# Pairs of chunks in a macaron encoder: two of four weight sums by accumulating transfers between slots, a bias table gathered in long rows, and later sums on GpSimd

## The chip, the cores and the metric

The kernel runs on one core of one Trainium2 chip. TensorE (PE) multiplies, VectorE (DVE) and ScalarE (ACT) prepare operands and evict results, GpSimd (POOL) does small sums and issues some transfers, SyncE (SP) issues the weight loads. The metric is the time of one execution in microseconds, median over runs. Lower is better.

## What is computed

Two layers, 256 tokens, model width 1024. Each layer has a feed-forward stage, a mixing stage and a second feed-forward stage:

```python
for l in range(DEPTH):
    x = x + 0.5 * swiglu(rms_norm(x, ffn1_norm[l]), ffn1_w_gate[l], ffn1_w_up[l], ffn1_w_down[l])
    h = rms_norm(x, mix_norm[l])
    z = h @ w_in[l]                    # q, k, v of 8 heads, p of 4 pooling groups
    a = neighborhood_attention(q, k, v, rpb[l])      # adds rpb_f[:, dr_idx][:, :, dc_idx], then a column mask
    m = multiscale_pool(p, w_pool[l], pool_scale[l])
    x = x + jnp.concatenate([a, m], axis=-1) @ w_out[l]
    x = x + 0.5 * swiglu(rms_norm(x, ffn2_norm[l]), ffn2_w_gate[l], ffn2_w_up[l], ffn2_w_down[l])
return rms_norm(x, final_norm)
```

with `swiglu(h, wg, wu, wd) = (silu(h @ wg) * (h @ wu)) @ wd`, and a feed-forward width of 2816, which the kernel takes as 11 chunks of 256. All data are float32.

## The kernel before

**Split products.** Every float32 product is made of three products on TensorE: each operand is split into a rounded part ("hi") and the rest ("lo"), and PE computes hi·hi, hi·lo and lo·hi (lines 1382, 1383 and 1385). A weight unit of 128 x 2048 words lies raw in a slot `w_raw[s]`; ACT writes `w_hi[s]` from it (`split_hi`, line 655, two instructions of 1024 words; line 662, four of 512, where a gain is folded in), and DVE subtracts to get `w_lo[s]` (`split_lo`, lines 1009 and 1020). There are five slots: three through the whole kernel, called a, b and d in a feed-forward stage, and e and f in such stages only. SP loads a slot as soon as its last `lo` is done.

**A feed-forward stage** (four of them: FF1 and FF2 of two layers) begins with chunk 0 and 1 in the ordinary way, then runs a loop of two bodies (`ff_body`), each of which handles one ordinary chunk and one *pair* of chunks, and ends with two more chunks. A pair is computed by seven half-size products in place of eight (`seventh` on PE), in the manner of Strassen and Winograd. For that it needs

- sums of the activations, made once a stage by POOL: `x_sums` first adds `xt_hi` and `xt_lo` back to the full value (line 504, two instructions of 1024 words), ACT scales the result by the gains (`scale_x`, line 749, eight instructions, which need both sums) and rounds it (`x_hi`, line 758), DVE makes the rest (`x_lo`, line 1096); then POOL makes four sums of blocks (lines 515 to 524, in place), which ACT and DVE split again (`s_hi`, `s_lo`, line 1107);
- four sums of weights for each pair. With raw units in e, f, b and a: the first sum is `e += f` on DVE (`add_units(e, f)`, line 1123), the second `b += e` on DVE, the third adds b's original words to f: POOL issues two transfers from DRAM that accumulate into slot f (`add_load`, line 532), and the fourth is `a += b` on DVE.

**The order at the start of a stage.** Every engine works through its own instructions in the written order. ACT: the splits of a's and b's second units (chunk 1), the split of d's first unit, `scale_x`, `store_gt_hi` of chunk 0 (line 729), `x_hi`, then chunk 1's silu. DVE: a's second unit, b's second unit (line 1020, four instructions each), d's first unit, `store_gt_lo` of chunk 0 (line 1076), `x_lo`, then chunk 1's gate, the third units of a and b, `s_lo`, and the first unit of the loop. PE: the products of chunk 1, then the down projection of chunk 0, which needs `gt_lo` of chunk 0, then chunk 2 with the scaled activations `xs`, the down projection of chunk 1, and the first `seventh`. POOL starts `x_sums` as soon as the transposed activations are complete (semaphore `xt_lo_ready`).

**The order in a pair.** PE: seventh e, seventh f, seventh a, seventh b, then seventh e with the second sum (called S2 here), a down projection, seventh f with the third sum, seventh a with the fourth, then the ordinary products from e and f. DVE's order around S2 is shown with the change.

**The bias.** The attention bias is 8 heads x 6 row distances x 64 columns per partition. It is gathered from `rpb` by `gather_rows` (line 551) on POOL's queue: 16 transfers a layer whose source runs backwards along the partitions, four heads' transfers in each loop body of FF1 and FF2 of layer 0, into a DRAM scratch; `load_bias` (line 559) fetches it to `bias` after the first feed-forward stage, and DVE applies the mask in place (line 1265).

## Time and profile before

| | |
|---|---|
| median of 3 runs | 937.91 us (934.59 to 942.03) |
| the profiled execution | 933.16 us, its span 931.4 us |
| PE busy | 913.9 us, 98% of the span |
| DVE busy | 702.2 us, 75% |
| ACT busy | 540.1 us, 58% |
| POOL busy | 116.5 us, 13% |
| granted TensorE clock | 0.998 of full speed |
| transfers | 184.3 MB, 198 GB/s on average |

A row of the profile is a group of instructions or one instruction: its line, the engine, the operation, what it writes and reads, how often, busy time, and the idle time of the engine before it with the instruction that ended it. Matmuls are pipelined: each of 512 columns shows a duration of about 0.39 us, while they start 0.2275 us apart when nothing is waited for, so the distance between starts is what to read, and a busy PE is no proof that PE runs without pauses.

### The profile page before, as it was taken

Reading aid. Unit: us, or ns where it says so; the run is one execution under the profiler, and the core shown is the slowest. Engines: PE = TensorE matmul, PEld = TensorE weight load, DVE = VectorE, ACT = ScalarE, POOL = GpSimd, SP = SyncE. Lnnn points to the kernel's source line nnn. Section 1 sums busy time; section 2 is a strip of 40 time slices with the busy share of each in tenths; the row PEclk is TensorE's granted clock in tenths of the full one; section 3 lists DMA queues with packets and bytes.
Section 4 is the critical chain, followed back from the end, with each engine's and each line's share of the span. In section 5 each row is a group of like instructions: output and inputs, shape, how many; then the busy total and the mean of one; then the engine's idle time right before and its main releaser. Section 6 shows DMA issues by size and latency. Waiting matters only on the chain.

```text
span 931.4 us, 12711 instructions
## 1 busy us (share of the span) xinstructions
PE 913.9 (98%) x4217; PEld 738.7 (79%) x4217; DVE 702.2 (75%) x898; ACT 540.1 (58%) x793; POOL 116.5 (13%) x124
## 2 busy tenths in 40 slices
PE   8999999999999999999999999999999999999997
PEld 6787877887778887887888878878877878778786
DVE  5999398468766998598379986874687479968854
ACT  6775365456647666365376655553775486546543
POOL 2310110110003311110033101000100033001000
PEclk9999999999999999999999999999999999999999
DMA  7868977975234968978558568658434277666641
GB/s 249 306 135 235 222 170 230 267 250 202 90 124 159 314 117 236 259 190 210 145 187 310 115 217 284 197 179 304 131 143 139 88 269 218 211 225 161 225 158 46
DMA packets 132412, 184.30 MB, mean 198 GB/s; under 512 B 8672, under 2 KB 108176, under 8 KB 132112
## 3 DMA queue, kind: packets, MB, share of 16 engines
q1 hardware_dynamic: 117744, 165.43, 52.0%
q0 software_dynamic: 11296, 14.77, 11.8%
q10 hardware_dynamic: 3328, 3.54, 1.1%
q8 instruction: 25, 0.41, 0.2%
q14 instruction: 19, 0.16, 0.1%
HBM read 182.58 MB, written 4.19 MB: 201 GB/s over the span
## 4 chain that ended last, share of the span: by engine, by line
PE 65%; DVE 8%; ACT 5%; issue 4%; DMA 4%; POOL 1%; DVEq 0%; SPq 0%; ACTq 0%; POOLq 0%
PE ps L1382 19%; PE ps L1385 19%; PE ps L1383 18%; DMA w_raw<-in_ffn_w_down_dram 4%; DVE w_lo_f L1009 2%; DVE w_raw L1123 2%; DVE w_lo L1009 1%; PE ps L1491 1%; PE ps L1443 1%; PE ps L1392 1%; PE ps L1393 1%; PE ps L1465 1%; PE ps L1679 1%; ACT w_hi L655 1%; ACT w_hi_f L671 1%
## 5 line engine op out<-in xcount | busy, mean ns | idle before, releaser
L1009 DVE TENSOR_TENSOR w_lo<-w_raw,w_hi 128x1024 fp32r<-128x1024 f32 x200 | 250.0, 1295 | 81.7 <-ACT w_hi L655 81.6
L655 ACT ACTIVATE w_hi<-w_raw 128x1024 fp32r<-128x1024 f32 x184 | 183.0, 1050 | 82.6 <-PE ps L1385 49.2
L1382 PE MATMUL ps<-w_hi,gt_hi 128*128 128x512 f32 (+1 forms) x356 | 140.1, 394 | 3.0 <-DVE w_lo L1009 1.7
L1383 PE MATMUL ps<-w_lo,gt_hi 128*128 128x512 f32 (+1 forms) x356 | 137.9, 387 | 0.0
L1382 PE MATMUL ps<-w_hi,xs_hi 128*128 128x512 f32 x288 | 114.0, 396 | 0.0
L1382 PE MATMUL ps<-w_hi,xt_hi 128*128 128x512 f32 x272 | 110.8, 407 | 2.6 <-DVE w_lo L1020 2.1
L1385 PE MATMUL ps<-w_hi,xs_lo 128*128 128x512 f32 x288 | 112.4, 390 | 0.0
L1383 PE MATMUL ps<-w_lo,xs_hi 128*128 128x512 f32 x288 | 112.2, 390 | 0.0
L1385 PE MATMUL ps<-w_hi,gt_lo 128*128 128x512 f32 (+1 forms) x356 | 109.9, 387 | 0.0
L1020 DVE SCALAR_TENSOR_TENSOR w_lo<-w_raw,gains,w_hi 128x512 fp32r<-128x512 f32 x128 | 94.1, 791 | 19.3 <-ACT w_hi L662 16.1
L1383 PE MATMUL ps<-w_lo,xt_hi 128*128 128x512 f32 x272 | 106.2, 391 | 0.0
L1385 PE MATMUL ps<-w_hi,xt_lo 128*128 128x512 f32 x272 | 101.2, 391 | 0.0
L662 ACT ACTIVATE w_hi<-w_raw,gains 128x512 fp32r<-128x512 f32 x120 | 76.6, 714 | 12.7 <-PE ps L1385 9.8
L1382 PEld LDWEIGHTS ps<-w_hi,gt_hi 128*128 128x128 f32 x356 | 66.8, 188 | 20.9 <-DVE w_lo L1009 5.0
L1385 PEld LDWEIGHTS ps<-w_hi,gt_lo 128*128 128x128 f32 x356 | 66.8, 188 | 13.9
L1383 PEld LDWEIGHTS ps<-w_lo,gt_hi 128*128 128x128 f32 x356 | 66.9, 188 | 12.9
L1382 PEld LDWEIGHTS ps<-w_hi,xt_hi 128*128 128x128 f32 x272 | 51.1, 188 | 19.8 <-issue 4.9
L1385 PEld LDWEIGHTS ps<-w_hi,xs_lo 128*128 128x128 f32 x288 | 54.0, 188 | 11.5
L1383 PEld LDWEIGHTS ps<-w_lo,xs_hi 128*128 128x128 f32 x288 | 54.2, 188 | 10.7
L1382 PEld LDWEIGHTS ps<-w_hi,xs_hi 128*128 128x128 f32 x288 | 54.1, 188 | 10.6
L729 ACT ACTIVATE gt_hi<-ps 128x512 fp32r<-128x512 f32 x40 | 23.6, 589 | 65.1 <-PE ps L1491 65.1
L1385 PEld LDWEIGHTS ps<-w_hi,xt_lo 128*128 128x128 f32 x272 | 51.0, 188 | 11.2
(146 smaller groups left out, 1524.8 us busy)
## 6 DMA issues: line engine op xcount, KB each, us to landing
w_raw<-in_ffn_w_down_dram SPq DMA_DIRECT2D x88, 512.0 KB, 6.5
w_raw<-in_ffn_w_gate_dram SPq DMA_DIRECT2D x54, 512.0 KB, 4.1
w_raw<-in_ffn_w_up_dram SPq DMA_DIRECT2D x54, 512.0 KB, 5.2
w_raw<-in_w_in_dram SPq DMA_DIRECT2D x32, 512.0 KB, 5.3
w_raw_e<-in_ffn_w_gate_dram SPq DMA_DIRECT2D x16, 512.0 KB, 4.9
w_raw_e<-in_ffn_w_up_dram SPq DMA_DIRECT2D x16, 512.0 KB, 6.6
w_raw_f<-in_ffn_w_gate_dram SPq DMA_DIRECT2D x16, 512.0 KB, 6.3
w_raw_f<-in_ffn_w_up_dram SPq DMA_DIRECT2D x16, 512.0 KB, 7.2
```

The source lines that it names most:

```text
L655: nc.scalar.activation(w_hi[slot][:, part], w_raw[raw][:, part], ACT.Copy).then_inc(hi_ready[slot], 2)
L662: nc.scalar.activation(w_hi[slot][:, part], w_raw[raw][:, part], ACT.Copy, scale=g).then_inc(hi_ready[slot], 1)
L671: nc.scalar.activation(w_hi[slot][:, part], w_raw[raw][:, part], ACT.Copy).then_inc(hi_ready[slot], 2)
L729: nc.scalar.activation(gt_hi[:, 0, :, :, :], ps[:, 6, :], ACT.Copy).then_inc(gt_hi_ready, 1)
L1009: nc.vector.tensor_tensor(w_lo[slot][:, part], w_raw[raw][:, part], w_hi[slot][:, part].bitcast(F32), ALU.subtract).then_inc(lo_ready[slot ...
L1020: nc.vector.scalar_tensor_tensor(w_lo[slot][:, part], w_raw[slot][:, part], g, w_hi[slot][:, part].bitcast(F32), ALU.mult, ALU.subtract).t ...
L1123: nc.vector.tensor_tensor(w_raw[into][:, :], w_raw[into][:, :], w_raw[other][:, :], ALU.add).then_inc(sum_ready, 1)
L1382: nc.tensor.matmul(o, hi, wh, start=start, stop=False)
L1383: nc.tensor.matmul(o, hi, wl, start=False, stop=False)
L1385: last = nc.tensor.matmul(o, lo, wh, start=False, stop=bool(stop))
L1392: nc.tensor.matmul(out, hi, w_hi_part, start=start, stop=False)
L1393: nc.tensor.matmul(out, hi, w_lo_part, start=False, stop=False)
```

## The change

It has three parts.

1. *Weight sums.* The second sum is now `e += b`, made by an accumulating transfer from slot b to slot e, which POOL issues once b's words are there and DVE is done with f's first unit of the pair (which reads e's raw words). The third, `f += b`, comes from slot b instead of from DRAM, and is issued after the second. DVE's fourth sum becomes `a += e`; it and the split of e now wait for the second transfer (`t2_loaded`). DVE's second sum is gone. SP waits for both transfers before it loads slot b again.
2. *Bias.* `gather_rows` issues two transfers a layer, of 256 rows of 250 words, after the first body's sums in FF1 of layer 0 and after the loop of FF2 of layer 0. `load_bias` fetches four pieces with overlapping rows into `q_t` and `k_t`, and the mask operation on DVE reads its words from there into `bias`. The stores of `q_t` and `k_t` now wait for the mask.
3. *GpSimd's sums.* `x_sums` waits in addition until DVE has finished b's second unit (`lo_ready[b]`).

```diff
@@ SP, loop body @@
-                    sp.wait_ge(sum_ready, 3 * pair_no(layer, ff, j) + 3)
+                    sp.wait_ge(t2_loaded, 16 * pair_no(layer, ff, j) + 16)
+                    sp.wait_ge(t3_loaded, 16 * pair_no(layer, ff, j) + 16)
+                    free(b, 2 * j + 4)
                     load_down(layer, weights, i + 2, b)
@@ POOL @@
                 pool.wait_ge(xt_lo_ready, number * 4 + 4)
+                b = ff["g"][1]
+                pool.wait_ge(lo_ready[b], 4 * unit_no(layer, ff["stage"], b, 1) + 5)
...
-            def add_load(layer, weights, i, a, slot, done):
...
+            def add_slot(slot, other, done):
+
+                pool.dma_start(w_raw[slot][:, :], w_raw[other][:, :], accum_op=ALU.add,
+                               max_dma_last_dim=4096).then_inc(done, 16)
+
+            def weight_sums(layer, ff, j):
+
+                b, e, f = ff["g"][1], SLOT_E, SLOT_F
+                pool.wait_ge(raw_ready[b], raw_count(b, raw_no(layer, ff["stage"], b, 3 * j + 3)))
+                pool.wait_ge(lo_ready[f], 4 * unit_no(layer, ff["stage"], f, 3 * j) + 5)
+                add_slot(e, b, t2_loaded)
+                pool.wait_ge(sum_ready, 2 * pair_no(layer, ff, j) + 1)
+                add_slot(f, b, t3_loaded)
+
+            def gather_rows(layer):
+
+
+                first = layer * N_HEADS * rpb_head + (WIN_ROWS - 4) * RPB_ROW + WIN_COLS - 1
+                for half in range(2):
+                    src = bass.AP(rpb.tensor, first + 4 * half * rpb_head,
+                                  [[rpb_head, 4], [-1, GRID_W], [1, SPAN + RPB_ROW]])
+                    pool.dma_start(bias_dram[layer, 4 * half:4 * half + 4, :, :], src
+                                   ).then_inc(bias_rows_loaded, 16)
@@ ACT, loop body @@
-                sum_hi(e, b, (sum_ready, 3 * n + 2), (m_ready, 7 * n + 1))
+                sum_hi(e, e, (t2_loaded, 16 * n + 16), (m_ready, 7 * n + 1))
...
-                sum_hi(f, f, (t3_loaded, 32 * n + 32), (m_ready, 7 * n + 2))
+                sum_hi(f, f, (t3_loaded, 16 * n + 16), (m_ready, 7 * n + 2))
...
-                sum_hi(a, a, (sum_ready, 3 * n + 3), (m_ready, 7 * n + 3))
+                sum_hi(a, a, (sum_ready, 2 * n + 2), (m_ready, 7 * n + 3))
@@ DVE, loop body @@
-                dve.wait_ge(lo_ready[b], 4 * unit_no(layer, ff["stage"], b, 2 * j + 3) + 5)
-                dve.wait_ge(sum_ready, 3 * n + 1)
-                add_units(b, e)
                 lo(d, 3 * j + 2, d)
-                lo(e, 3 * j + 1, b)
+                dve.wait_ge(t2_loaded, 16 * n + 16)
+                dve.wait_ge(lo_ready[a], 4 * unit_no(layer, ff["stage"], a, 4 * j + 3) + 5)
+                add_units(a, e)
+                lo(e, 3 * j + 1, e)
...
-                dve.wait_ge(sum_ready, 3 * n + 2)
-                add_units(a, b)
```

On POOL the change begins at the start of the first feed-forward stage. Before, with the two sums of line 504, the four of block sums, and then the accumulating loads and the first of the gathers:

```order
L504 TENSOR_TENSOR normed<-xt_hi,xt_lo 128x1024 [waits xt_lo_ready]
L504 TENSOR_TENSOR normed<-xt_hi,xt_lo 128x1024
L515 TENSOR_TENSOR normed<-normed 128x512 [waits x_lo_ready]
L518 TENSOR_TENSOR normed<-normed 128x512 [waits s_summed]
L521 TENSOR_TENSOR normed<-normed 128x512 [waits s_summed]
L524 TENSOR_TENSOR normed<-normed 128x512 [waits s_summed]
L532 DMA w_raw_f<-in_ffn_w_gate_dram 128x4x256 [waits raw_ready4,sum_ready]
L532 DMA w_raw_f<-in_ffn_w_up_dram 128x4x256
L551 DMA bias_scratch<-in_rpb_dram 6x64x64 [waits down_used]
L551 DMA bias_scratch<-in_rpb_dram 6x64x64
```

The same place after the change (`lo_ready1` counts what DVE has finished of slot b, `lo_ready4` of slot f):

```order
L514 TENSOR_TENSOR normed<-xt_hi,xt_lo 128x1024 [waits lo_ready1,xt_lo_ready]
L514 TENSOR_TENSOR normed<-xt_hi,xt_lo 128x1024
L525 TENSOR_TENSOR normed<-normed 128x512 [waits x_lo_ready]
L528 TENSOR_TENSOR normed<-normed 128x512 [waits s_summed]
L531 TENSOR_TENSOR normed<-normed 128x512 [waits s_summed]
L534 TENSOR_TENSOR normed<-normed 128x512 [waits s_summed]
L539 DMA w_raw_e<-w_raw 128x2x1024 [waits lo_ready4,raw_ready1]
L539 DMA w_raw_f<-w_raw 128x2x1024 [waits sum_ready]
L558 DMA bias_scratch<-in_rpb_dram 256x1x250 x2
```

The sums have one wait more, the loads from DRAM have become transfers between slots of which the first waits for DVE's split of f, and the gathers are two.

On DVE the change is in the middle of the loop body, between the split of b and the store of `gt_lo`. Before (`w_raw` is slot b in the row of line 1123):

```order
L1009 TENSOR_TENSOR w_lo<-w_raw,w_hi 128x1024 [waits hi_ready1]
L1148 REGISTER_ALU
L1123 TENSOR_TENSOR w_raw<-w_raw,w_raw_e 128x2048 [waits sum_ready,lo_ready1]
L1008 ISA
L1009 TENSOR_TENSOR w_lo<-w_raw,w_hi 128x1024 [waits hi_ready2]
L1008 REGISTER_ALU
L1009 TENSOR_TENSOR w_lo<-w_raw,w_hi 128x1024 [waits hi_ready2]
L1009 TENSOR_TENSOR w_lo_e<-w_raw,w_hi_e 128x1024 [waits hi_ready3] x2
L1076 TENSOR_TENSOR gt_lo<-ps,gt_hi 128x512 [waits gt_hi_ready]
```

The same place after the change (`w_raw` is slot a in the row of line 1134):

```order
L1020 TENSOR_TENSOR w_lo<-w_raw,w_hi 128x1024 [waits hi_ready1]
L1019 ISA
L1020 TENSOR_TENSOR w_lo<-w_raw,w_hi 128x1024 [waits hi_ready2]
L1019 REGISTER_ALU
L1020 TENSOR_TENSOR w_lo<-w_raw,w_hi 128x1024 [waits hi_ready2]
L1160 ISA
L1161 REGISTER_ALU [waits t2_loaded]
L1134 TENSOR_TENSOR w_raw<-w_raw,w_raw_e 128x2048 [waits lo_ready0]
L1020 TENSOR_TENSOR w_lo_e<-w_raw_e,w_hi_e 128x1024 [waits hi_ready3] x2
L1087 TENSOR_TENSOR gt_lo<-ps,gt_hi 128x512 [waits gt_hi_ready]
```

One sum of 2048 words has left this place, and another has moved to it from further down, between the wait for the transfer and the split of e. The orders of ACT at the start of a stage and of PE everywhere are the same as before.

## Rows read from the trace of the kernel before

**Rows 1.** Page, part 1: busy us, share of the span, instructions.
```profile
PE 913.9 (98%) x4217; PEld 738.7 (79%) x4217; DVE 702.2 (75%) x898; ACT 540.1 (58%) x793; POOL 116.5 (13%) x124
```

**Rows 2.** Waits of PE: who waited for whom: us, times, longest.
```profile
PE ps L1491 <- DVE w_lo_f L1009: 2.5, 8, 0.3
PE ps L1382 <- DVE w_lo L1020: 2.1, 2, 1.8
PE ps L1382 <- DVE w_lo L1009: 1.7, 8, 0.2
PE ps L1382 <- DVE w_lo_e L1009: 1.6, 5, 0.4
PE ps L1382 <- DVE gt_lo L1076: 1.4, 1, 1.4
```

**Rows 3.** Timeline of DVE, FF2 of layer 0: start, us, instruction, [idle before].
```profile
294.36 3.79 DVE L1020 SCALAR_TENSOR_TENSOR w_lo<-w_raw,gains,w_hi 128x512 fp32r<-128x512 f32 x4 [1.00 <-ACT w_hi L662]
...
298.47 2.73 DVE L1020 SCALAR_TENSOR_TENSOR w_lo<-w_raw,gains,w_hi 128x512 fp32r<-128x512 f32 x4
301.12 2.34 DVE L1009 TENSOR_TENSOR w_lo<-w_raw,w_hi 128x1024 fp32r<-128x1024 f32 x2
304.80 0.69 DVE L1076 TENSOR_TENSOR gt_lo<-ps,gt_hi 128x512 fp32r<-128x512 f32 x1 [1.33 <-ACT gt_hi L729]
305.75 2.36 DVE L1096 TENSOR_TENSOR xs_lo<-normed,xs_hi 128x1024 fp32r<-128x1024 f32 x2 [0.26 <-ACT xs_hi L758]
...
324.15 0.68 DVE L1076 TENSOR_TENSOR gt_lo<-ps,gt_hi 128x512 fp32r<-128x512 f32 x1
```

**Rows 4.** Timeline of ACT, the same stretch.
```profile
300.98 3.30 ACT L749 ACTIVATE normed<-normed,gains 128x256 f32<-128x256 f32 x8
```

**Rows 5.** Timeline of POOL, the same stretch.
```profile
290.86 4.75 POOL L504 TENSOR_TENSOR normed<-xt_hi,xt_lo 128x1024 f32<-128x1024 f32 x2
```

**Rows 6.** Timeline of PE: first matmuls of the first two down projections of FF2.
```profile
308.08 0.39 PE L1382 MATMUL ps<-w_hi,gt_hi 128*128 128x512 f32 x1
...
324.99 0.49 PE L1382 MATMUL ps<-w_hi,gt_hi 128*128 128x512 f32 x1
```

**Rows 7.** Timeline of DVE in the first pair of FF2, layer 0.
```profile
328.66 2.36 DVE L1009 TENSOR_TENSOR w_lo_f<-w_raw_e,w_hi_f 128x1024 fp32r<-128x1024 f32 x2 [1.24 <-ACT w_hi_f L671]
...
336.10 2.29 DVE L1123 TENSOR_TENSOR w_raw<-w_raw,w_raw_e 128x2048 f32<-128x2048 f32 x1
...
340.58 2.35 DVE L1009 TENSOR_TENSOR w_lo_e<-w_raw,w_hi_e 128x1024 fp32r<-128x1024 f32 x2
```

**Rows 8.** Timeline of PE in that pair: first matmul of S2.
```profile
341.93 0.42 PE L1382 MATMUL ps<-w_hi_e,xs_hi 128*128 128x512 f32 x1
```

**Rows 9.** DMA issues (KB each, median us to landing); queue 0 in 331 to 336 us.
```profile
w_raw_f<-in_ffn_w_gate_dram POOLq DMA_DIRECT2D x8, 512.0 KB, 6.4
w_raw_f<-in_ffn_w_up_dram POOLq DMA_DIRECT2D x8, 512.0 KB, 8.3
...
q0 software_dynamic: 973, 0.98, 123.2%
```

**Rows 10.** Timelines of DVE and PE at the start of FF1, layer 0.
```profile
26.09 2.72 DVE L1020 SCALAR_TENSOR_TENSOR w_lo<-w_raw,gains,w_hi 128x512 fp32r<-128x512 f32 x4
...
32.48 2.36 DVE L1096 TENSOR_TENSOR xs_lo<-normed,xs_hi 128x1024 fp32r<-128x1024 f32 x2 [0.25 <-ACT xs_hi L758]
...
50.88 0.68 DVE L1076 TENSOR_TENSOR gt_lo<-ps,gt_hi 128x512 fp32r<-128x512 f32 x1
...
52.47 0.39 PE L1382 MATMUL ps<-w_hi,gt_hi 128*128 128x512 f32 x1
```

**Rows 11.** Timelines in the second pair of FF1, layer 1: split of f, S2.
```profile
576.87 2.36 DVE L1009 TENSOR_TENSOR w_lo_f<-w_raw_e,w_hi_f 128x1024 fp32r<-128x1024 f32 x2 [1.25 <-ACT w_hi_f L671]
...
593.80 0.39 PE L1382 MATMUL ps<-w_hi_e,xs_hi 128*128 128x512 f32 x1
```

**Rows 12.** Waits of all engines: ACT for loads of the down projection.
```profile
ACT w_hi L655 <- DMA w_raw<-in_ffn_w_down_dram: 26.9, 3, 11.1
```

More of the change, by code:

```diff
@@ L201, in trunk, with spans @@
         A11, A12, A21, A22, S2, S4, S3, S1 = range(N_OPERANDS)
+        def spans(half):
+            tile = (q_t, k_t)[half]
+            return tile[:, :, :, :].rearrange("p g t q -> p (g t q)")[:, 0:4 * SPAN]
         def diff_t(g):
@@ L224, in trunk @@
         sum_ready = sem("sum_ready")
+        t2_loaded = sem("t2_loaded")
         t3_loaded = sem("t3_loaded")
@@ L556, in load_bias @@
             def load_bias(layer):
                 pool.wait_ge(gu_ready[1], ord_no(layer, FF1, 2 * BODIES + 1) + 1)
-                pool.wait_ge(bias_rows_loaded, 16 * 2 * N_HEADS * (layer + 1))
-                pool.dma_start(bias[:, :, :, :].rearrange("p h d c -> p (h d c)"),
-                               bias_dram[layer, :, :]).then_inc(bias_loaded, 16)
+                pool.wait_ge(bias_rows_loaded, 32 * (layer + 1))
+                for half in range(2):
+                    for rq in range(P // GRID_W):
+                        shift = (1 - rq) * RPB_ROW
+                        src = bias_dram[layer, 4 * half:4 * half + 4, :, shift:shift + SPAN]
+                        dst = spans(half)[rq * GRID_W:(rq + 1) * GRID_W, :]
+                        pool.dma_start(dst.rearrange("p (h s) -> p h s", h=4),
+                                       src.rearrange("h p s -> p h s")).then_inc(bias_loaded, 16)
@@ L562, in _ @@
             pool.wait_ge(eps_ready, 1)
             rstd_of(0)
-            first, second = (ffn1_w_gate, ffn1_w_up), (ffn2_w_gate, ffn2_w_up)
             x_sums(0, FF1)
             for j in range(BODIES):
-                weight_sums(0, FF1, first, j)
-                gather_rows(0, FF1, 0, j)
+                weight_sums(0, FF1, j)
+                if j == 0:
+                    gather_rows(0)
             load_bias(0)
@@ L573, in _ @@
             for j in range(BODIES):
-                weight_sums(0, FF2, second, j)
-                gather_rows(0, FF2, 1, j)
+                weight_sums(0, FF2, j)
+            gather_rows(1)
             rstd_of(3)
@@ L578, in _ @@
             for j in range(BODIES):
-                weight_sums(1, FF1, first, j)
+                weight_sums(1, FF1, j)
             load_bias(1)
@@ L584, in _ @@
             for j in range(BODIES):
-                weight_sums(1, FF2, second, j)
+                weight_sums(1, FF2, j)
             last = STAGES * DEPTH
@@ L906, in mix_stage @@
                 mix_unit(layer, 5)
+                act.wait_ge(bias_masked, layer + 1)
                 for h in range(2):
@@ L1260, in mix_stage @@
                 mix_unit(layer, 3)
[L1262 removed]
+                dve.wait_ge(bias_loaded, layer * 64 + 64)
                 for h in range(0, N_HEADS, 2):
[L1264 removed]
+                    pair = spans(h // 4)
+                    words = bass.AP(pair.tensor, pair.offset + h % 4 * SPAN,
+                                    [list(pair.ap[0]), [SPAN, 2], [RPB_ROW, DELTAS], [1, GRID_W]])
                     done = nc.vector.tensor_tensor(
[L1266 to L1267 removed]
+                        bias[:, h:h + 2, :, :], words,
+                        mask[:, :].rearrange("p (o e c) -> p o e c", o=1, e=1)
+                        .to_broadcast([P, 2, DELTAS, GRID_W]), ALU.min)
                 done.then_inc(bias_masked, 1)
@@ L1275, in mix_stage @@
                 mix_unit(layer, 6)
+                dve.wait_ge(bias_masked, layer + 1)
                 for h in range(2):
```

37 lines of the change are left out of this document (5 added, 32 removed).

## The prediction

> **What bounds the kernel now.** The page comes first: PE is busy for 98% of the span and no other engine for more than 79% [rows 1]. PE works in one fixed order, which the change leaves as it is, so whatever PE waits for is added to the time, and only removing a wait can shorten it. The waits of PE, read next, are small: 9.3 us in all in the five large groups [rows 2]. They are of three kinds. One wait of 1.8 us and a small one stand at the start of FF1 in layer 0, where DVE splits with gains (line 1020). One of 1.4 us is for `gt_lo`. The others, 2.5 + 1.7 + 1.6 us, stand at the end of the eight pairs. After each wait the next matmul starts some 0.15 us late, so all of them together are worth about 12 us, and no more than that can be gained.
>
> Then the timelines of DVE, ACT, POOL and PE at the start of FF2 in layer 0, since part 3 of the change acts there, and last those of the first pair, where part 1 acts.
>
> **Part 3, the later sums.** What they disturb now: DVE's split of a's second unit takes 3.79 us for four instructions where the next four take 2.73 [rows 3]. POOL's two sums run to 295.61 [rows 5], and the split began at 294.36, so DVE's first instruction stood until POOL's had ended; 1.06 us. PE waited little for that in three of the four stages, and 2.1 us in FF1 of layer 0 [rows 2].
>
> What the new wait does, step by step, in FF2 of layer 0. The split of b's second unit ended at 301.20 [rows 3]; with 1.06 us less before it, at 300.1. POOL starts at 300.2 in place of 290.86. Its sums take 4.75 us [rows 5]. But DVE is by then at its next split, d's first unit, two instructions of 1.17 us (301.12, 2.34 us [rows 3]), and the two engines were seen to stand for each other; with POOL first, one of these lies between the two sums: 5.9 us, end at 306.1. `scale_x` needs both sums and takes 3.30 us [rows 4]: it ends at 309.4, where it ended at 304.28. That is 5.1 us later, and ACT has `store_gt_hi` and `x_hi` behind it.
>
> - `gt_lo` ended at 305.49, 1.21 us after `scale_x` [rows 3, 4]; now at 310.6. PE's first down projection began at 308.08 [rows 6], and would stand for 2.6 us.
> - `x_lo` began 1.47 us after `scale_x` [rows 3, 4], so it too is 5.1 us later. From there to the end of `gt_lo` of chunk 1 at 324.83 DVE was never idle [rows 3], since POOL's four block sums and the splits they slow are in this stretch. PE took up that result at 324.99 [rows 6], only 0.16 us later. So PE is late by 5.1 - 0.16 = 4.9 us there, the first 2.6 included; I take 5.0 with the restarts.
>
> The two starts in layer 1 have the same distances: 3 x 5.0 = 15.0 us. In FF1 of layer 0, b's split ended at 28.81 [rows 10], and without the disturbance, which cost PE 2.1 us and two restarts there [rows 2], at about 26.4. Then 5.9 + 3.3 + 1.47 + 2.36 us lead to the end of `x_lo` at 39.5, against 34.84 [rows 10]: 4.7 us later. Here the slack was larger, 52.47 - 51.56 = 0.9 [rows 10], so PE loses 3.8 us, the wait that goes away already counted. **Part 3: +18.8 us.** What hid these sums before was the early time, 290.86 to 295.61, in which DVE and ACT had little to do; that cover is gone.
>
> **Part 1, the transfer.** In the first pair f's first split ends at 331.02 [rows 7]; POOL issues 0.2 us later. PE took up S2 at 341.93 [rows 8], and the first half of e's split had ended at 341.8 (340.58 plus half of 2.35 [rows 7]): no slack. In the new order the fourth sum (2.29 us, as the row of 336.10 [rows 7]) stands between the transfer's end and that split. To be in time the transfer must have landed at 341.9 - 1.2 - 2.3 = 338.4, that is 7.2 us after its issue. No row shows one between slots. The nearest are the accumulating loads that it replaces: 0.5 MB landed in 6.4 us [rows 9]. Queue 0 moved 0.98 MB in 5 us while they ran, 196 GB/s [rows 9], so 2.7 of the 6.4 us were transfer and 3.7 fixed, and 1.05 MB in one piece needs 3.7 + 5.4 = 9.1 us. From below: at twice that rate, 6.4 us, S2 is not late at all. From above: at half the rate, 14.5 us. I take 9.1, as the nearest row has the same kind of transfer: PE stands at S2 for 9.1 - 7.2 = 1.9, with the restart 2.0 us.
>
> This holds for the first pair of each stage, whose DVE and PE are tied by the stage's start. In the second pair of a stage PE comes later: in FF1 of layer 1 f's split ended at 579.23 and S2 began at 593.80, 14.6 us behind against 10.9 in the first pair [rows 7, 8, 11]. There the transfer has 3.6 us more and hides. In layer 0 the second pairs were late because ACT waited up to 11.1 us for a load [rows 12], while the gathers of part 2 were under way; with long rows that goes, and the 1.4 us for `gt_lo` with it. So S2 costs 4 x 2.0 = **+8.0 us**.
>
> Behind `t2_loaded` stand, on DVE, the splits of e and f and the combinations; the third transfer lands 5.4 us after the second, at about 345.7, ACT rounds the first half by 346.8, and PE reaches S3 36 matmuls after S2's start at 343.9, at 352.1: hidden. On SP the load into slot b waits for 345.7, where it waited for the fourth sum, which DVE made behind the splits of e and f, at 342.93 + 2.35 + 2.29 = 347.6 at the earliest: not later.
>
> Saved: the waits for e's last split, 1.6 us in five pairs [rows 2] and five restarts, 2.3 us, since DVE has one sum less (8 x 2.29 us); and `gt_lo`'s, 1.5. **-3.8 us.** The waits for f's and a's last splits stay (2.5 and 1.7 us, eight times each [rows 2]): they occur also in the second pairs, where DVE has time, so they hang on the chain from PE's own last product through combination and split, which no part shortens.
>
> **Part 2** is hidden but for what it does to the loads. The mask reads from other tiles for the same time, the stores of `q_t` wait for it a microsecond or two long before PE reads them, and four issues for one lie in a stretch where POOL waits.
>
> **Sum:** 18.8 + 8.0 - 3.8 = +23.0 us. On the profiled execution's span of 931.4 that is 954.4, and on its time of 933.2, 956. The median of the runs is 4.7 us above this execution; by it, 961. I say 959.
>
> **The Trainium skill.** Its page "DMA: Bandwidth & Descriptors", section "Anatomy of one DMA — SWDGE (gpsimd) path", gives such a transfer about 2.0 us and its bytes over 436 GB/s, an estimate of 4.4 us here. By it S2 would never be late and the sum would be +15; the accumulating loads of this trace, 6.4 us for half the bytes [rows 9], speak against it. Its page "SBUF — State Buffer", section "Who interferes with whom", says that an operation of DVE with two inputs in SBUF and one of GpSimd that reads SBUF exclude each other for a whole instruction, and that the order of issue decides who stands. The trace agrees [rows 3, 5].
>
> **The rivals.**
>
> - *DVE first.* The split of d's first unit and POOL's first sum become free within 0.1 us of each other. With DVE first both its instructions lie before the last sum, and each later start costs 1.2 us more: +3.5 us, 962. It is inside my forecast.
> - *The sums hide* (the other side). If POOL's sums did not delay `scale_x` beyond PE's slack, part 3 would gain 2.4 us in layer 0 and lose nothing, and with a transfer in time the whole change would give -2.4 - 3.8 = -6.2: 932. It decides at one point: `gt_lo` of chunk 0 has 308.08 - 305.49 = 2.6 us of slack, so the sums would have to end by 303.6, yet their wait ends at 300.1 and they need 4.75 alone. For it speaks only that POOL's start can't be seen in advance.
> - *Half of it.* The starts cost only the first down projection's 2.6 us each, as DVE would catch up behind (the block sums fall where DVE is free), or the transfer lands within 7.2 us: +8 to +15 us, 941 to 950.
> - *The transfer is slow.* At half the rate it lands at 14.5 us: 7.3 us late in four pairs and some 3.7 in four: +44 in place of +8, 990 or more. At three quarters, 10.9 us: +7, 966.
>
> **Chances.** The forecast with DVE first, 950 to 970: 0.57. Half of it, 941 to 950: 0.16. The sums hide, partly or wholly, 928 to 941: 0.19, of which 0.07 below 929. The slow transfer, over 970: 0.08. The range 941 to 970 leaves out some 2 in 10 on both sides, the larger part below. A measurement of this kernel tells apart about 1%: faster than 928.5 has 0.07, slower than 947.3 has 0.75, the rest 0.18.
>
> **What would show it.** Right: in the profile after, a wait of PE for `gt_lo` (line 1087) of 2 to 4 us at the first down projection of each of four stages; `scale_x` idle on POOL's `normed` before it; first matmul of S2 waiting for e's split in the first pairs, by about 2 us; the accumulating transfer at 9 us from issue to landing. The waits for f's and a's last split are unchanged. Wrong: no wait at the first down projection, which would mean that `scale_x` or the sums run in another order or faster than here; or a landing under 7.2 us, which takes 8 us off.

## The result: 956.4 us against 940.0, ratio 1.018

| | before | after |
|---|---|---|
| median | 939.97 us (934.59 to 942.59, 4 runs) | 956.43 us (956.33 to 956.55, 4 runs) |
| ratio | | 1.018, 95% interval 1.013 to 1.023 |
| span of the profiled execution | 931.4 us | 954.5 us |
| granted TensorE clock, mean | 0.998 | 0.988 |

The kernel is slower, by more than the 1% that can be told apart. On the spans it is 23.1 us, by these medians 16.5. The kernel before scatters: its medians over the 7 to 21 runs beside the experiments are 934.7 to 936.1, and against those the change costs 20.3 to 21.7 us.

**Page of the kernel after, part 1** (busy us, share of the span, instructions); before is [rows 1]:

```profile
PE 921.1 (96%) x4217; PEld 745.0 (78%) x4217; DVE 690.1 (72%) x890; ACT 539.7 (57%) x793; POOL 102.3 (11%) x102
```

PE has the same 4217 instructions. DVE lost the eight sums and is less busy, and the time went up all the same.

**Waits of PE after** (who waited for whom: us in all, times, longest); before is [rows 2]:

```profile
PE ps L1394 <- DVE gt_lo L1087: 15.6, 4, 4.1
PE ps L1394 <- DVE w_lo_e L1020: 4.3, 4, 1.4
PE ps L1503 <- DVE w_lo_f L1020: 2.5, 8, 0.3
PE ps L1394 <- DVE w_lo L1020: 2.3, 10, 0.3
...
PE ps L1394 <- DVE w_lo L1031: 0.3, 1, 0.3
```

A new wait for `gt_lo` stands at each of the four stage starts, 3.5 us in FF1 of layer 0 and 4.05 in the others, and one of 0.9 to 1.4 us at S2 in the four first pairs. The 2.1 us at the splits with gains (line 1031, before line 1020) are down to 0.3. The waits for f's and a's last splits are as before; the row of ten holds a's eight (1.7 us) and two of 0.3 us at stage starts.

**Timelines after, start of FF2 in layer 0**, of POOL, DVE, ACT and PE (start, us, instruction, [idle before]); before are [rows 3 to 6]. By this place the kernel after is already 3.5 us late: its split of a's second unit begins at 297.90, before's at 294.36. Differences to rows of before have to be lessened by that.

```profile
297.90 2.74 DVE L1031 SCALAR_TENSOR_TENSOR w_lo<-w_raw,gains,w_hi 128x512 fp32r<-128x512 f32 x4 [1.00 <-ACT w_hi L672]
...
303.83 6.77 POOL L514 TENSOR_TENSOR normed<-xt_hi,xt_lo 128x1024 f32<-128x1024 f32 x2 [9.38 <-DVE w_lo L1031]
...
303.79 4.56 DVE L1020 TENSOR_TENSOR w_lo<-w_raw,w_hi 128x1024 fp32r<-128x1024 f32 x2
314.45 0.69 DVE L1087 TENSOR_TENSOR gt_lo<-ps,gt_hi 128x512 fp32r<-128x512 f32 x1 [6.10 <-ACT gt_hi L739]
...
310.64 3.30 ACT L759 ACTIVATE normed<-normed,gains 128x256 f32<-128x256 f32 x8 [6.01 <-POOL normed L514]
...
315.19 0.79 PE L1394 MATMUL ps<-w_hi,gt_hi 128*128 128x512 f32 x1 [4.05 <-DVE gt_lo L1087]
...
320.48 0.56 PE L1394 MATMUL ps<-w_hi,gt_hi 128*128 128x512 f32 x1
...
333.76 0.68 DVE L1087 TENSOR_TENSOR gt_lo<-ps,gt_hi 128x512 fp32r<-128x512 f32 x1
...
334.75 0.39 PE L1394 MATMUL ps<-w_hi,gt_hi 128*128 128x512 f32 x1
```

DVE began first (303.79 against 303.83), and its two instructions, 2.34 us by themselves [rows 3], took 4.56, POOL's two 6.77 in place of 4.75. `scale_x` then waited for the sums, `gt_lo` of chunk 0 for `scale_x`, and PE for `gt_lo`. The second down projection starts at 334.75 in place of 324.99: 9.8 us later, 6.2 of them from this stage.

The two starts in layer 1 look the same, with DVE ahead by 0.04 and 0.05 us. In FF1 of layer 0 it is the other way round, POOL begins 0.6 us ahead, and its sums take 5.75 us:

```profile
26.55 5.75 POOL L514 TENSOR_TENSOR normed<-xt_hi,xt_lo 128x1024 f32<-128x1024 f32 x2 [7.69 <-DVE w_lo L1031]
27.14 6.24 DVE L1020 TENSOR_TENSOR w_lo<-w_raw,w_hi 128x1024 fp32r<-128x1024 f32 x2 [0.74 <-ACT w_hi L665]
```

**Windows after, the same stretch** (from and to; its length; busy us and instructions of PE, PEld, DVE, ACT, POOL; granted clock; DMA share; GB/s):

```profile
300.00:310.80 10.80, 10.80 (x51) 8.86 (x50) 8.25 (x8) 4.79 (x8) 6.77 (x2) 1.00 0.82 273
310.80:315.20 4.40, 0.35 (x3) 0.01 (x1) 0.69 (x1) 4.40 (x10) 0.00 (x0) 0.86 1.02 380
315.20:317.00 1.80, 1.80 (x4) 1.48 (x5) 1.60 (x2) 1.80 (x4) 0.00 (x0) 0.50 0.91 321
317.00:319.00 2.00, 2.00 (x6) 1.54 (x5) 2.00 (x3) 2.00 (x4) 1.17 (x1) 0.50 0.09 32
319.00:321.00 2.00, 2.00 (x6) 1.55 (x6) 2.00 (x2) 1.82 (x2) 1.92 (x2) 0.54 0.00 0
321.00:324.00 3.00, 3.00 (x15) 2.47 (x14) 3.00 (x3) 0.00 (x0) 2.84 (x3) 1.00 0.07 15
```

I had not foreseen this. Behind the wait of 4 us the granted clock was 0.50, the lower of its two levels (1.2 GHz), for some 6 us, and matmuls started 0.43 us apart. The first down projection (24 matmuls) took 8.2 us, 315.19 to 323.39, where 24 starts at 0.2275 us are 5.5. It happened in all four starts, where the same 24 matmuls took 7.2 to 8.2 us. Whether these 1.8 to 2.8 us a start, 8.8 in all, are part of the loss is the question of three experiments below.

**Timelines after, first pair of FF2**, of POOL, DVE and PE; before are [rows 7, 8]:

```profile
341.21 1.25 POOL L539 DMA_DIRECT2D w_raw_e<-w_raw  x1 [15.39 <-DVE w_lo_f L1020]
...
338.28 2.36 DVE L1020 TENSOR_TENSOR w_lo_f<-w_raw_e,w_hi_f 128x1024 fp32r<-128x1024 f32 x2 [1.25 <-ACT w_hi_f L681]
...
349.19 2.29 DVE L1134 TENSOR_TENSOR w_raw<-w_raw,w_raw_e 128x2048 f32<-128x2048 f32 x1 [1.34 <-DMA w_raw_e<-w_raw]
...
352.67 0.50 PE L1394 MATMUL ps<-w_hi_e,xs_hi 128*128 128x512 f32 x1 [0.91 <-DVE w_lo_e L1020]
```

**DMA issues after** (count, KB each, median us from issue to landing); before is [rows 9]:

```profile
w_raw_e<-w_raw POOLq DMA_DIRECT2D x8, 1024.0 KB, 7.9
w_raw_f<-w_raw POOLq DMA_DIRECT2D x8, 1024.0 KB, 12.6
```

The transfer landed 7.9 us after its issue, 8.5 us after f's split (ended 340.64), and held up the fourth sum and with it e's split and S2.

### The profile page after: what moved, and what is told of

The parts are those of the page before. It is cut to its first block, busy times and chain, and to the rows that moved or that the text cites. A ratio compares the mean times of both kernels' runs of the same rounds, so it can differ in the third digit from the quotient of the medians.

```text
span 954.5 us, 12695 instructions
## 1 busy us (share of the span) xinstructions
PE 921.1 (96%) x4217; PEld 745.0 (78%) x4217; DVE 690.1 (72%) x890; ACT 539.7 (57%) x793; POOL 102.3 (11%) x102
## 4 chain that ended last, share of the span: by engine, by line
PE 65%; DVE 10%; POOL 6%; DMA 6%; issue 6%; ACT 5%; SPq 1%; DVEq 0%; ACTq 0%; POOLq 0%
PE ps L1394 19%; PE ps L1397 18%; PE ps L1395 18%; DMA w_raw_f<-w_raw 4%; POOL normed L514 3%; DVE w_lo L1031 2%; DVE w_lo_f L1020 2%; DVE w_lo_e L1020 2%; DVE w_lo L1020 1%; PE ps L1503 1%; ACT normed L759 1%; DMA w_raw<-in_ffn_w_up_dram 1%; DVE xs_lo L1107 1%; PE ps L1455 1%; PE ps L1404 1%
## 5 line engine op out<-in xcount | busy, mean ns | idle before, releaser
L1020 DVE TENSOR_TENSOR w_lo<-w_raw,w_hi 128x1024 fp32r<-128x1024 f32 x200 | 259.5, 1348 | 70.3 <-ACT w_hi L665 70.0
L1394 PE MATMUL ps<-w_hi,gt_hi 128*128 128x512 f32 (+1 forms) x356 | 144.0, 404 | 17.4 <-DVE gt_lo L1087 15.6
L1395 PE MATMUL ps<-w_lo,gt_hi 128*128 128x512 f32 (+1 forms) x356 | 141.2, 397 | 0.0
L1397 PE MATMUL ps<-w_hi,gt_lo 128*128 128x512 f32 (+1 forms) x356 | 112.6, 395 | 0.0
L1031 DVE SCALAR_TENSOR_TENSOR w_lo<-w_raw,gains,w_hi 128x512 fp32r<-128x512 f32 x128 | 88.0, 746 | 17.6 <-ACT w_hi L672 15.3
L1394 PEld LDWEIGHTS ps<-w_hi,gt_hi 128*128 128x128 f32 x356 | 68.9, 193 | 37.4 <-DVE gt_lo L1087 17.3
L1397 PEld LDWEIGHTS ps<-w_hi,gt_lo 128*128 128x128 f32 x356 | 68.8, 193 | 14.6
L1395 PEld LDWEIGHTS ps<-w_lo,gt_hi 128*128 128x128 f32 x356 | 69.0, 194 | 13.5
L1087 DVE TENSOR_TENSOR gt_lo<-ps,gt_hi 128x512 fp32r<-128x512 f32 x40 | 27.6, 689 | 63.2 <-ACT gt_hi L739 63.2
```

What stands on the lines that cost most here:

```text
L1020: nc.vector.tensor_tensor(w_lo[slot][:, part], w_raw[raw][:, part], w_hi[slot][:, part].bitcast(F32), ALU.subtract).then_inc(lo_ready[slot ...
L1031: nc.vector.scalar_tensor_tensor(w_lo[slot][:, part], w_raw[slot][:, part], g, w_hi[slot][:, part].bitcast(F32), ALU.mult, ALU.subtract).t ...
L1087: nc.vector.tensor_tensor(gt_lo[:, 0, :, :, :].rearrange("p k t q -> p (k t q)"), ps[:, 6, :], gt_hi[:, 0, :, :, :].rearrange("p k t q -> ...
L1394: nc.tensor.matmul(o, hi, wh, start=start, stop=False)
L1395: nc.tensor.matmul(o, hi, wl, start=False, stop=False)
L1397: last = nc.tensor.matmul(o, lo, wh, start=False, stop=bool(stop))
```

## Experiments

The kernel before ran beside each group of experiments on the same chip, with medians of 935.8 (e1 to e4), 936.1 (e5 to e7, and again e8 to e10) and 934.7 us (e12). The four groups ran on four chips; the same kernel on two of them (e3, e10) differs by 0.1 us. Times of the kernel before scatter by 5 to 11 us from run to run, those of most of the others by 0.2 to 2, so parts are compared among these.

### 1. The three parts apart

*e1*: the changed kernel without the additional wait of GpSimd's sums (parts 1 and 2).

```diff
                 pool.wait_ge(xt_lo_ready, number * 4 + 4)
-                b = ff["g"][1]
-                pool.wait_ge(lo_ready[b], 4 * unit_no(layer, ff["stage"], b, 1) + 5)
```

> The changed kernel with the wait of GpSimd's first sums for b's second unit taken out, so the new transfers and the long gathers alone. If the later sums are what costs, the waits for gt_lo (15.6 us) and the slow stretches behind them go, and the time comes back to that of the kernel before: some 18 us under the changed kernel, ratio to before 0.995 to 1.003. If the transfers between slots are the cost, it stays at 1.01 or more, with waits for e's split in all eight pairs.

*e2*: the same two lines added to the kernel before (part 3 alone).

> The kernel before with only that wait added. If the later sums explain the loss alone, +16 to +20 us on before, ratio 1.017 to 1.022, with four waits of PE for gt_lo of 3.5 to 4.2 us. If part of the loss needs the new transfers too (their queue on GpSimd, or transfers that land later), less than +12 us.

*e3*: the kernel before with the new `gather_rows`, `load_bias` and mask operation (part 2 alone).

> The kernel before with only the bias gathered in long rows and masked from q_t and k_t. If the old gathers only delayed loads, the wait of PE for gt_lo (1.4 us) goes and ACT's waits for loads of the down projection (26.9 us) nearly vanish: -1 to -3 us, within 0.4% of before. Rival: the gathers also lengthen the weights' loads elsewhere on the path, and more than 4 us are gained.

*e8*: e3 with the wait of e2 (parts 2 and 3), and *e10*: e3 once more, beside e8.

> The kernel before with the long bias gathers and the full delay of GpSimd's sums, so the changed kernel without the transfers between slots. The later sums alone cost 25.6 us on the kernel before, but 22.8 us between the changed kernel and the one without the delay. Theory A (the parts add; the extra 3 us of the delay alone came from the old short gathers, whose transfers were in flight at the first layer's down projections and gave waits of 1.0, 0.5 and 1.1 us there): 953 to 954, and the difference to the changed kernel is the price of the transfers, 2.5 to 3.5 us. Theory B (with late sums the transfers between slots win time that they don't win with early ones, since they take a sum off VectorE while it is behind): 956 to 958, level with the changed kernel or above.

> The kernel before with the long bias gathers alone, once more, beside the two others on the same chip: 930.5, ratio 0.9955 to the kernel before, within 1 us.

| kernel | parts | us, median | ratio to before, 95% interval |
|---|---|---|---|
| e3 | 2 | 930.47 | 0.9955 (0.9940 to 0.9969) |
| e10 | 2 | 930.36 | 0.9945 (0.9925 to 0.9965) |
| e1 | 1, 2 | 933.59 | 0.9979 (0.9964 to 0.9995) |
| e2 | 3 | 961.38 | 1.0295 (1.0253 to 1.0337) |
| e8 | 2, 3 | 952.77 | 1.0182 (1.0160 to 1.0204) |
| after | 1, 2, 3 | 956.43 | 1.0183 (1.0133 to 1.0233) |

Part 3 costs 22.4 us over part 2 (e8 against e10) and 22.8 over parts 1 and 2 (after against e1; I had expected 18). Part 1 costs 3.1 us with early sums (e1 against e3) and 3.7 with late ones (after against e8). The parts add within 0.6 us, and theory A of e8 holds, with 952.8 just under its 953. Part 2 gains some 5 us by the medians, past the 4 us of e3's rival, and 3.0 by the spans (928.4 against 931.4), the end of what I expected. The kernel before scatters by more than these two figures differ, so this experiment does not decide between the two.

Part 3 on the kernel before costs 25.6 us by the medians, more than the 22.4 and more than I expected. The four runs of e2 lie in two pairs (957.5 and 958.2, 964.6 and 965.0), so its median is rough; by the spans it is 24.3 (955.7 against 931.4) where e8 has 22.2 over e10. Waits of PE in e2:

```profile
PE ps L1384 <- DVE gt_lo L1078: 16.8, 6, 4.1
...
PE ps L1384 <- ACT normed L775: 0.9, 1, 0.9
```

and in e8:

```profile
PE ps L1395 <- DVE gt_lo L1086: 15.6, 4, 4.1
```

With the old gathers there are two more waits for `gt_lo`, one each in FF1 and FF2 of layer 0, and one for `normed` in that FF2. The one in FF1 the kernel before has too (1.4 us). With the starts of the same matmuls set against each other, e2 falls 2.6 us further behind e8 in FF2 of layer 0 after the stage's start, the kernel before only 0.5 behind e10, and elsewhere the two differences are alike. These 2.1 us are the difference of the spans, and lie where the second layer's old gathers run, which e8 doesn't have.

### 2. Is it the first wait and the slow clock, or the late chain?

Both experiments start from the changed kernel. *e5* lets ACT make `gt_hi` of chunk 0 ahead of `scale_x`, so that the first down projection doesn't depend on the sums:

```diff
-                scale_x(layer, ff)
                 store_gt_hi(layer, ff, 0)
+                scale_x(layer, ff)
                 x_hi(layer, ff)
```

> The changed kernel, with ScalarE's store_gt_hi of chunk 0 put ahead of scale_x, so that gt_lo of chunk 0 no longer waits for the later sums: TensorE's 4 us wait before the first down projection should be gone in all four stages, and with it the stretch at half clock behind it. Two theories of where the 6 us per stage come from. Theory A (the late chain decides): the sums end at about 310.6, scale_x, x_hi, x_lo, the splits of a's and b's third units and gt_lo of chunk 1 follow one another on ScalarE and VectorE without a pause, and they stay as late as before; TensorE runs through the first down projection and chunk 2's first half and waits later, at w_lo of the third units or at gt_lo of chunk 1, for about as long in sum: at most 1 to 2 us per stage won, time 948 to 956 on a kernel of 956. Theory B (the first wait and the slow clock behind it cost the time, what follows has slack): some 4 us of wait and what the slow clock takes are saved, 5 to 6 us per stage, time 932 to 938.

*e6* fills the wait with 16 matmuls whose result nothing reads:

```diff
+                for n in range(16):
+                    nc.tensor.matmul(ps[:, 2, :], zeros[:, 0:P], zeros[:, :], start=True, stop=True)
                 whole_down(layer, ff, 0, d, 0, first=True)
```

> The changed kernel, with 16 additional matmuls of 512 columns (zeros, into a bank that is free then, 3.6 us at full clock) on TensorE ahead of the first down projection of each feed-forward stage: they fill the stretch in which TensorE waits, so the granted clock should stay at 1.0 behind it (before this it fell to 0.50 for 3.4 to 6.8 us in each of the four stages). The wait itself remains, only filled. Theory A (the late chain on ScalarE and VectorE decides, the slow clock only fills time in which TensorE would wait for it): TensorE now goes through the first down projection at 5.6 us instead of 8.4 and then waits about as much longer at w_lo of the third units or at gt_lo of chunk 1; time unchanged within 2 us. Theory B (the slow clock itself costs time): 2 to 2.8 us per stage are saved, 8 to 11 us in all, time 945 to 949.

Measured: e5 954.65 us (954.46 to 954.76), 1.8 less than the changed kernel, and e6 956.36 (956.04 to 957.54), the same as the changed kernel. Theory A holds in both.

Timelines of e5, FF2 of layer 0, PE and then DVE:

```profile
310.45 0.39 PE L1394 MATMUL ps<-w_hi,gt_hi 128*128 128x512 f32 x1
...
319.40 0.50 PE L1394 MATMUL ps<-w_hi,xs_hi 128*128 128x512 f32 x1 [3.34 <-DVE w_lo L1020]
...
333.71 0.49 PE L1394 MATMUL ps<-w_hi,gt_hi 128*128 128x512 f32 x1
...
314.55 2.36 DVE L1107 TENSOR_TENSOR xs_lo<-normed,xs_hi 128x1024 fp32r<-128x1024 f32 x2 [6.12 <-ACT xs_hi L768]
...
332.87 0.68 DVE L1087 TENSOR_TENSOR gt_lo<-ps,gt_hi 128x512 fp32r<-128x512 f32 x1
```

The first down projection no longer waits, and PE now stands 3.3 us at the next place, chunk 2, for the split of the third unit, since DVE still makes `x_lo` after the late sums (314.55 here, 315.40 after). The second down projection starts 1.0 us sooner than in the changed kernel, not 4, and 0.5 of that it had already when the stage began.

Windows of e6 in the same stretch, and its PE and DVE at the two down projections:

```profile
308.00:315.00 7.00, 6.56 (x30) 5.12 (x29) 0.71 (x2) 4.69 (x11) 2.27 (x1) 1.00 1.06 384
315.00:321.00 6.00, 6.00 (x27) 4.96 (x28) 5.93 (x5) 5.50 (x8) 3.41 (x2) 1.00 0.23 83
321.00:335.00 14.00, 12.57 (x54) 9.14 (x53) 13.96 (x13) 6.64 (x8) 4.34 (x3) 1.00 0.66 213
...
314.88 0.50 PE L1394 MATMUL ps<-w_hi,gt_hi 128*128 128x512 f32 x1 [0.44 <-DVE gt_lo L1087]
...
324.41 0.50 PE L1394 MATMUL ps<-w_hi,xs_hi 128*128 128x512 f32 x1 [0.58 <-DVE w_lo L1020]
326.64 0.50 PE L1394 MATMUL ps<-w_hi,xs_hi 128*128 128x512 f32 x1 [0.57 <-DVE w_lo L1020]
...
334.29 0.49 PE L1394 MATMUL ps<-w_hi,gt_hi 128*128 128x512 f32 x1
...
333.45 0.68 DVE L1087 TENSOR_TENSOR gt_lo<-ps,gt_hi 128x512 fp32r<-128x512 f32 x1
```

The clock stays at 1.00, and the mean over the run is 0.999. PE goes through the down projection at full speed and then waits for the splits of the third units instead. In both kernels the second down projection starts just behind `gt_lo` of chunk 1: 0.16 us behind its end in e6, 0.31 in the changed kernel. The slow clock lay in time that PE would have waited. It was a near thing: in FF2 of layer 0 of the changed kernel PE waits nowhere between the two down projections, so its own path (the first wait and the slow clock) and the late chain end within 0.15 us of each other. Taking away the first wait or the slow clock alone gains next to nothing. Shortening the chain alone, with the first wait left, was not tried, nor was a version without all three.

### 3. A threshold, or a price per microsecond?

*e7* is e3 with GpSimd's sums waiting for a's second unit in place of b's:

```diff
                 pool.wait_ge(xt_lo_ready, number * 4 + 4)
+                a = ff["g"][0]
+                pool.wait_ge(lo_ready[a], 4 * unit_no(layer, ff["stage"], a, 1) + 5)
```

> The kernel before with the gathering of the bias in long pieces (the part that made it faster by itself, 930.5 against 935.8), and with GpSimd's sums waiting for a's second unit instead of for b's: they start some 7 us later than before and some 8 us earlier than in the changed kernel (at about 295.8 in FF2 of layer 0, end at about 300.6, just when ScalarE comes to scale_x). My theory (the sums cost time only by what they end later than ScalarE is ready for them, a threshold and not a rate): no wait at the first down projection over 0.5 us, time within 2 us of 930.5. The rival (each us of delay costs a share, by contention of the sums with the splits of b's and d's units, or because later sums are later at x_lo): about half of the 25 us that the full delay cost, 940 to 944.

Measured: 945.00 us (944.14 to 947.80), 14.5 above e3. My theory fell: there is no wait at the first down projection, as it said, but the time is lost some 11 us ahead of it (that projection starts at 314.68). Timelines of e7 (POOL, DVE, PE):

```profile
298.09 5.17 POOL L511 TENSOR_TENSOR normed<-xt_hi,xt_lo 128x1024 f32<-128x1024 f32 x2 [6.34 <-DVE w_lo L1030]
...
298.25 6.88 DVE L1030 SCALAR_TENSOR_TENSOR w_lo<-w_raw,gains,w_hi 128x512 fp32r<-128x512 f32 x4
...
301.08 0.50 PE L1395 MATMUL ps<-w_hi,xt_hi 128*128 128x512 f32 x1 [1.30 <-DVE w_lo L1030]
303.86 0.80 PE L1395 MATMUL ps<-w_hi,xt_hi 128*128 128x512 f32 x1 [1.81 <-DVE w_lo L1030]
```

and the same split of DVE in e3, where POOL's sums run while a's second unit is split:

```profile
296.11 2.73 DVE L1028 SCALAR_TENSOR_TENSOR w_lo<-w_raw,gains,w_hi 128x512 fp32r<-128x512 f32 x4
```

b's split takes 6.88 us in place of 2.73, and PE, which is just about to use it, stands twice, for 1.3 and 1.8 us. Under a's split, in e3, the same sums leave no wait over 0.4 us in three of the four stages. So it is not a threshold. The rival was nearer, with 940 to 944 and with contention of the sums with b's split as one of its reasons, but it isn't a share of each microsecond of delay either: the price depends on which split the sums fall upon and how soon PE needs it.

The waits are 3.1 us a start, the loss is more. Window of e7 behind them:

```profile
304.00:309.00 5.00, 5.00 (x14) 4.02 (x15) 3.40 (x4) 2.63 (x8) 0.00 (x0) 0.50 0.52 147
```

PE again runs at half clock. I set the starts of the same matmuls in e7 and e3 against each other: e7 is 3.2 us late ahead of this place, 6.15 behind the two waits, 8.95 forty matmuls later, where PE waits for nothing, and still 8.75 at the second down projection. Here the slow clock seems to cost 2.8 us in this start. *e12* tests it with fillers in the two waits of e7:

```diff
+                def fill(count):
+                    for n in range(count):
+                        nc.tensor.matmul(ps[:, 2, :], zeros[:, 0:P], zeros[:, :], start=True, stop=True)
...
-                    ordinary(layer, ff, 1, t, ff["g"], (1, 1), scaled=False)
+                    ordinary(layer, ff, 1, t, ff["g"], (1, 1), scaled=False,
+                             after={3: lambda: fill(7), 4: lambda: fill(9)} if t == 0 else {})
```

> The kernel e7 (long bias gathers, GpSimd's sums waiting for a's second unit, 945.0 us) with fillers on TensorE in its two waits for b's second unit: 7 matmuls of 512 columns on zeros (1.6 us) ahead of that unit's products and 9 (2.0 us) behind its first three. In the trace of e7 the granted clock is 0.50 from about 304 to 309 us, after the two waits of 1.3 and 1.8 us. Set matmul by matmul against the version without the delayed sums, TensorE is 3.19 us late ahead of this place, 6.15 behind the two waits and 8.95 forty matmuls later, where it waits for nothing: so by this theory the slow clock itself cost 2.8 us in each of three starts, because here VectorE and ScalarE are not behind. With the fillers the clock stays at 1.00 and 8 us are saved: 936 to 938. Rival: the slow clock lies in time that TensorE would have waited anyway, as in the changed kernel: 944 to 946.

Measured: 938.29 us (937.93 to 938.71), 6.7 less than e7. The same window of e12:

```profile
304.00:309.00 5.00, 5.00 (x25) 4.14 (x24) 4.75 (x6) 4.91 (x8) 0.10 (x1) 1.00 0.93 289
```

Set against e3 in the same way, e12 is 1.3 us late ahead of this place, 4.4 behind the waits, 4.45 forty matmuls later: the waits cost what they did, the stretch behind them nothing. So in e7 the slow clock cost some 6 to 7 of the 14.5 us (6.7 by the medians, 5.8 by the spans, 942.3 against 936.5), a little less than the 8 I expected, and in the changed kernel, where e6 took it away too, nothing. It was not in every start: 2.6 us of it lie in FF2 of layer 0 and about 1.5 in each FF1, while in FF2 of layer 1 the same two waits of 1.3 and 1.8 us left the granted clock of e7 at 1.00. The difference to the changed kernel is whether the other engines are late behind the wait: there they were, in e7 they were not.

### 4. The order at S2

*e4* is e1 with DVE's split of e ahead of the fourth sum (`a += e`), and SP's load into e waiting for that sum:

```diff
+                lo(e, 3 * j + 1, e)
+                store_gt_lo(layer, ff, i)
                 dve.wait_ge(t2_loaded, 16 * n + 16)
                 dve.wait_ge(lo_ready[a], 4 * unit_no(layer, ff["stage"], a, 4 * j + 3) + 5)
                 add_units(a, e)
-                lo(e, 3 * j + 1, e)
-                store_gt_lo(layer, ff, i)
```

> The kernel of e1 with DVE's split of e and the store of gt_lo ahead of the fourth sum, and SP's next load of e behind that sum. If S2 is late only because the fourth sum (2.29 us) stands between the transfer and the split, PE's waits for w_lo_e at S2 go and the time is 3 to 6 us under e1. If the transfer itself is late, at most 1 us is gained; if the later load of e hurts, waits for e's last split come back.

Measured: 932.36 us (931.43 to 933.08), 1.2 less than e1, where I had expected 3 to 6. Waits of PE in e1 and in e4:

```profile
PE ps L1392 <- DVE w_lo_e L1018: 3.2, 4, 1.0
```

```profile
PE ps L1392 <- DVE w_lo_e L1018: 1.6, 4, 0.6
```

S2 no longer waits, as meant. The wait for e's last split, which the changed order had removed, came back in the first pairs (the 1.6 us stand there), as the fourth sum now lies between. I had named such a return as a sign that the later load of e hurts; which of the two it is was not separated.

### 5. A version that beats both

In e3, PE's four transposes of `gated_x` stand behind the wait for f's last split. *e9* puts them ahead of it:

```diff
-                ordinary(layer, ff, 2 * j + 3, 0, (e, f), units, {4: transpose_x})
+                ordinary(layer, ff, 2 * j + 3, 0, (e, f), units, after={3: transpose_x})
```

> The kernel before with the long bias gathers, and in each pair TensorE's four transposes of gated_x moved in its program from behind the wait for f's last split to ahead of it. In the version with the bias alone they start at 357.08, when that split's first half is done (356.94), while their input was ready at 355.80 and TensorE had been free since 356.59: so they should start 0.45 us sooner and lie in the wait. If the last split of a, 3.6 us behind, follows (its input waits for what the transposes feed), 0.3 to 0.4 us per pair are saved, 2.4 to 3.3 us in all: 927 to 928. Rival: a's split does not come sooner, since VectorE is busy until 359.1, and TensorE waits there for what it gained: 930 to 931.

Measured: 927.95 us (927.01 to 928.18), ratio to before 0.9912 (0.9893 to 0.9932); e10 in the same call 930.36. PE in a first pair of e3:

```profile
357.08 0.65 PE L1502 MATMUL ps<-ident,gated_x 128*128 128x128 f32 x4 [0.33 <-DVE w_lo_f L1017]
...
360.70 0.50 PE L1393 MATMUL ps<-w_hi,gt_hi 128*128 128x512 f32 x1 [0.22 <-DVE w_lo L1017]
```

and of e9:

```profile
357.19 0.60 PE L1502 MATMUL ps<-ident,gated_x 128*128 128x128 f32 x4
...
360.82 0.50 PE L1393 MATMUL ps<-w_hi,gt_hi 128*128 128x512 f32 x1 [0.25 <-DVE w_lo L1017]
```

The wait at the transposes is gone in all eight pairs, the one at a's last split stays. The 2.4 us are the lower end of what I expected: 0.3 per pair.

## Why the prediction came out right

I had said +23.0 us on the span, 956 on the profiled execution and 959 by the medians; measured were +23.1, 956.35 and 956.4. The sum is closer than its terms, and that is luck: part 3 came out 3.4 us dearer than forecast, part 1 was 2.1 cheaper and part 2 gained 1.5 more. By the spans of after, e8, e10 and e3, and of the kernel before:

| term | predicted | measured |
|---|---|---|
| part 3, later sums | +18.8 | +22.2 (e8 950.9 - e10 928.7) |
| part 1, transfer, less e's last split | +8.0 - 2.3 = +5.7 | +3.6 (after 954.5 - e8 950.9) |
| part 2, bias | -1.5 | -3.0 (e3 928.4 - before 931.4) |

The measured terms add to 22.8; the other 0.3 lies between the spans of e10 and e3, which are the same kernel.

- **Part 3, place and chain: right.** The waits stand at the first down projection of the four stages, `scale_x` idles on POOL's sums, and PE takes up the second down projection 0.16 to 0.31 us behind the end of `gt_lo` of chunk 1. That the later chain is enough to hold PE there without the first wait is shown by e5, and without the slow clock by e6.
- **Part 3, size: the order of the two engines was wrong in three of four starts.** I let POOL begin (5.9 us for its sums) and named DVE first as a rival: both of DVE's instructions before the last sum, 1.2 us more in each of the three later starts, +3.5 in all. That is what happened: there DVE began 0.04 us ahead and the sums took 6.77 us, while in FF1 of layer 0 POOL began and they took 5.75. 18.8 + 3.5 = 22.3 is the measured price. Stage by stage, with the starts of the same matmuls in e8 and e10 set against each other, the cost is 4.0 us in FF1 of layer 0 and 6.0 to 6.1 in each of the others, where the forecast with this order is 3.8 and 6.2. The sign of 0.04 us couldn't be read from the trace of before. Saying so, and pricing both orders, was the most that could be done.
- **The size of the first wait was too small.** I had 2.6 us, or 3.8 with DVE first; PE lost 4.2, and 3.6 in FF1 of layer 0. The end of `gt_lo` was forecast well. PE came to the place sooner: set against e3, whose sums are early, the kernel after is 5.9 us late when FF2 begins and 5.3 just ahead of this wait, so the early sums had cost PE 0.6 us there that I had called little and left out. It changed nothing in the sum, because the chain behind has the last word.
- **The slow clock was not foreseen**, and cost nothing that can be measured, by e6. That was luck: in e7 the same clock cost 6 to 7 us (e12), and had the chain behind the wait been shorter the forecast would have been low.
- **Part 1, the transfer: right in kind, too large.** It landed in 7.9 us, I had 9.1 from an accumulating load of half the size. It was issued 0.57 us after f's split, I had 0.2. Together 8.5 us instead of 9.3, against the 7.4 us of room: 1.1 us late. PE lost 1.1 to 1.5 us in each of the four first pairs, 4.9 us in all where I had 8.0, and none in the second pairs, as said. The term mis-sized is the fixed 3.7 us, got from a load from DRAM: the 5.4 us for the bytes fit, as the next transfer of the same size landed 5.5 us behind this one. The Trainium skill's page "DMA: Bandwidth & Descriptors", section "Anatomy of one DMA — SWDGE (gpsimd) path", would have 4.4 us, as an estimate; the measured 7.9 is far from it.
- **Saved waits: mostly right.** The wait for e's last split is gone in all pairs, though two of the five went by part 2 (next point). f's and a's stay as before, 2.5 and 1.7 us in eight waits each, in every version but e9, which fits that they hang on PE's own last product; e9 takes away the first kind by moving PE's own work.
- **Part 2: under.** I counted only the wait of 1.4 us for `gt_lo` in layer 0. It went, as said, and so did ACT's waits for loads of the down projection [rows 12]. The other 1.5 us on the spans are, with the starts of the same matmuls in the kernel before and e10 set against each other, some 0.5 us in the second pair of each stage of layer 0, where PE's wait for e's last split is gone as well, 0.2 more at the `gt_lo` place, and the 0.3 between e3 and e10. By the medians part 2 gives some 5 us; the profiled execution of before, 933.16 us, was faster than all but two of its runs beside the experiments.
- **The rivals.** "The sums hide" and "half of it" fell with the 22.2 us of part 3 and the wait in four of four starts. "The transfer is slow" fell with the 7.9 us.

Open: why the kernel before scatters by 5 to 11 us in its runs, and e2 by 7.6, while the versions with long gathers scatter by 0.2 to 3.7. The short gathers are the difference, but no run here shows how they act.

## What to carry to other kernels

When a side engine's work is moved, ask two things: upon which instruction of a shared-memory neighbour it will fall, and how soon the bound engine needs that instruction. In this kernel the same two sums cost little under one split, 14.5 us over four stages under the next (6 to 7 of them by the slow clock), and 22 us behind it. When two engines come free at the same time, price both orders, and look behind the first wait to the last link of the chain: removing the first wait alone (e5) gave back 1.8 of 22 us. A wait of some microseconds on TensorE can have a second price, the slow clock behind it, and in these runs it was paid only where nothing else was late.
